# A chain of three transformer blocks on one core: two of the four weight sums of a block product move from VectorE to GpSimd

## The reference

```python
def conv_ffn(h, in_w, conv_w, conv_b, out_w):
    u = causal_dwconv(h @ in_w, conv_w, conv_b)
    g, v = jnp.split(u, 2, axis=-1)
    return (jax.nn.silu(g) * v) @ out_w
```

## Time and profile before

| what | value |
|---|---|
| median of 3 runs | 3161.73 us (3160.71 to 3162.06) |
| the profiled execution | 3163.01 us, its span 3161.2 us, granted TensorE clock 0.996 |
| PE matmuls busy | 3098.6 us, 98% of the span |
| DVE busy | 1332.4 us, 42% |
| ACT busy | 705.6 us, 22% |
| POOL busy | 286.0 us, 9% |
| feed-forward of layer 0, pairs 2 to 21 on PE | 399.73 to 527.41 us |
| feed-forward of layer 1, pairs 2 to 21 on PE | 867.27 to 995.03 us |

### The profile page before, as it was taken

One profiled execution on the slowest core, in us unless ns is written; L12 is line 12 of the kernel. 1 busy time (PEld: TensorE's weight loads), 2 busy tenths in 40 slices (PEclk: granted clock), 3 DMA queues, 4 the chain that ended last, 5 costly groups with the idle time before them and its releaser, 6 DMA issues.

```text
span 3161.2 us, 44989 instructions
## 1 busy us (share of the span) xinstructions
PE 3098.6 (98%) x18322; PEld 2420.7 (77%) x18322; DVE 1332.4 (42%) x2837; ACT 705.6 (22%) x1252; POOL 286.0 (9%) x240
## 2 busy tenths in 40 slices
PE   8999999999999999999999999999999999999998
PEld 7788899888899888998899988888455545544544
DVE  4632289473489455754367544444111111111111
ACT  3621121252221152102220133420111111111111
POOL 0210001070010100001100013200000000000000
PEclk9999999999999999999999999999999999999999
DMA  6543344433244433443254443236899999999996
GB/s 242 160 147 134 120 173 161 160 120 120 87 182 161 157 120 133 169 165 147 94 192 164 155 156 127 83 133 243 349 428 429 428 428 429 428 429 429 428 429 264
DMA packets 72725, 719.43 MB, mean 228 GB/s; under 512 B 8273, under 2 KB 8273, under 8 KB 10753
## 3 DMA queue, kind: packets, MB, share of 16 engines
q1 hardware_dynamic: 70704, 709.93, 56.6%
q0 software_dynamic: 1872, 7.38, 1.0%
HBM read 716.19 MB, written 1.08 MB: 227 GB/s over the span
## 4 chain that ended last, share of the span: by engine, by line
PE 85%; DMA 9%; DVE 4%; ACT 1%; issue 1%; POOL 0%; SPq 0%; DVEq 0%; POOLq 0%; ACTq 0%
PE bank L285 28%; PE bank L2379 11%; PE bank L1399 10%; PE bank L3553 10%; DMA weight_ring<-in_experts 9%; PE bank L304 8%; PE bank L3584 5%; PE bank L3538 3%; PE bank L3530 2%; PE bank L2677 1%; DVE residual L1144 1%; PE bank L487 0%; PE bank L1251 0%; PE bank L1231 0%; PE bank L1698 0%
## 5 line engine op out<-in xcount | busy, mean ns | idle before, releaser
L285 PE MATMUL bank<-normed_residual,weight_ring 128*128 128x256 f32 x2400 | 535.3, 381 | 0.0
L285 PEld LDWEIGHTS bank<-normed_residual,weight_ring 128*128 128x128 f32 x2400 | 452.6, 190 | 66.3 <-issue 7.2
L3637 DVE TENSOR_TENSOR arena<-bank,arena 128x512 f32<-128x512 f32 x32 | 22.1, 691 | 614.3 <-PE bank L3553 614.3
L285 PE MATMUL bank<-arena,weight_ring 128*128 128x256 f32 x1144 | 253.5, 381 | 4.7 <-ACT arena L1758 3.9
L285 PEld LDWEIGHTS bank<-arena,weight_ring 128*128 128x128 f32 x1144 | 217.4, 191 | 34.8 <-issue 4.3
L3553 PE MATMUL bank<-weight_ring,arena 128*64 128x512 f32 x1024 | 227.7, 593 | 3.1 <-DMA weight_ring<-in_experts 3.1
L3553 PE MATMUL bank<-arena 128*64 128x512 f32 x1024 | 225.2, 592 | 2.3 <-DVE arena L3631 2.3
L304 PE MATMUL bank<-gained_residual,weight_ring 128*128 128x256 f32 x896 | 204.2, 388 | 21.5 <-DVE gained_residual L378 12.0
L3584 PE MATMUL bank<-weight_ring,arena 128*64 128x512 f32 x992 | 219.7, 595 | 0.0
L304 PEld LDWEIGHTS bank<-gained_residual,weight_ring 128*128 128x128 f32 x896 | 174.2, 195 | 48.2 <-DVE gained_residual L378 14.0
L3553 PEld LDWEIGHTS bank<-weight_ring,arena 128*64 128x64 f32 x1024 | 72.6, 137 | 152.8 <-issue 138.9
(11 more groups left out here) (460 smaller groups left out, 4397.2 us busy)
## 6 DMA issues: line engine op xcount, KB each, us to landing
weight_ring<-in_stream SPq DMA_DIRECT2D x290, 1024.0 KB, 4.8
weight_ring<-in_experts SPq DMA_DIRECT2D x126, 2048.0 KB, 18.7
arena<-in_experts SPq DMA_DIRECT2D x66, 2048.0 KB, 18.9
arena<-rows POOLq DMA_DIRECT2D x8, 512.0 KB, 6.7
residual<-in_x SPq DMA_DIRECT2D x2, 512.0 KB, 6.3
arena<-in_mem POOLq DMA_DIRECT2D x1, 1024.0 KB, 5.1
out<-gained_residual SPq DMA_DIRECT2D x4, 256.0 KB, 2.3
arena<-in_p POOLq DMA_DIRECT2D x2, 256.0 KB, 2.8
```

What stands on the lines that cost most here:

```text
L285: mm = nc.tensor.matmul(PB[b][:, m * T:m * T + T], l, r, start=(kc == 0), stop=(kc == chunks - 1))
L3637: nc.vector.tensor_tensor(CHID, PB[1][:, :], CSILU, ALU.mult).then_inc(sem["hid_ready"], 1)
```

## The change

All pairs from 3 to 21 go through blocks now (19 of 22; pairs 8, 14 and 20 are new in each layer), so the second linear's units start at n = 19 in place of 16. For the first linear's units POOL makes sums 0 and 2 (ffn_sums_pool) and signals pair_sums; DVE waits for that and makes sums 1 and 3 alone. The second linear's units have all four sums on DVE as before.

```diff
-    return name[:6] == "ffn_in" and p > 2 and p % 6 != 2 or name[:7] == "ffn_out" and p < FFN_OUT_WHOLE
+    return name[:6] == "ffn_in" and p > 2 or name[:7] == "ffn_out" and p < FFN_OUT_WHOLE
...
+        def ffn_sums_pool(pool, l, n):
+
+            u, c = ffn_unit(l, n), FFN_UNITS[n][3]
+            w = W[:, u % SLOTS]
+            pool.wait_ge(arrived[u % SLOTS], 16 * (u // SLOTS + 1))
+            if n >= 2:
+                pool.wait_ge(sem["unit_used"], ffn_unit(l, n - 2) + 1)
+            nc.gpsimd.tensor_tensor(ffn_sums(l, n, 0), w[:, 0:c, hi], w[:, c:2 * c, hi], ALU.add).then_inc(sem["pair_sums"], 1)
+            nc.gpsimd.tensor_tensor(ffn_sums(l, n, 2), w[:, 0:c, lo], w[:, 0:c, hi], ALU.subtract).then_inc(sem["pair_sums"], 1)
+
         def ffn_sums_dve(dve, own, l, n):
...
-            if n >= 2:
+            if n < len(IN_PAIRS):
+                dve.wait_ge(sem["pair_sums"], 2 * len(IN_PAIRS) * l + 2 * n + 2)
+            else:
                 dve.wait_ge(sem["unit_used"], ffn_unit(l, n - 2) + 1)
-            own(nc.vector.tensor_tensor(ffn_sums(l, n, 0), w[:, 0:c, hi], w[:, c:2 * c, hi], ALU.add))
-            nc.vector.tensor_tensor(ffn_sums(l, n, 2), w[:, 0:c, lo], w[:, 0:c, hi], ALU.subtract)
-            own.wait()
+                own(nc.vector.tensor_tensor(ffn_sums(l, n, 0), w[:, 0:c, hi], w[:, c:2 * c, hi], ALU.add))
+                nc.vector.tensor_tensor(ffn_sums(l, n, 2), w[:, 0:c, lo], w[:, 0:c, hi], ALU.subtract)
+                own.wait()
...
             for q in range(11):
+                for p in range(0 if q == 0 else 2 * q + 3, min(2 * q + 5, 22)):
+                    if p in IN_PAIRS:
+                        ffn_sums_pool(pool, l, IN_PAIRS.index(p))
```

More of the change, by code:

```diff
@@ L200 @@
 mem1_ready swept_conv swept_gate conv_mm conv_out
-part_done second_in second_std hn_gate block_ready""".split()
+part_done pair_sums second_in second_std hn_gate block_ready""".split()
 def program(nc, io):
```

## The result

| kernel | median us | lowest to highest | runs |
|---|---|---|---|
| before | 3161.89 | 3160.71 to 3162.49 | 8 |
| changed | 3171.79 | 3170.17 to 3172.87 | 8 |

The ratio is 1.0029, 95% interval 1.0019 to 1.0038: slower by 9.9 us, where the prediction took 0.2% (6.3 us) as the limit of what can be told. No run of one kernel lies in the range of the other. The profiled execution of the changed kernel took 3172.87 us (span 3171.1), 9.86 us more than that of before.

The account below looks back on a forecast made before the run. PE was taken as the limit, with DVE barely keeping up. Terms -3.96 + 2.6 + 1.8 + 4.7 = +5.1 us on the median 3161.73 gave 3166.8 us, bounds 3163 to 3169, range 3161 to 3172.

Parts of the forecast that it names:

- longer POOL sums: Rival: POOL's sums take 1.58 us, not 1.26; starts wait longer, +2.6 us in all, 3169.4 us; chance 0.18.
- Three whole pairs a layer become block pairs: PE in the first linear, both layers: pairs of 6.25 us replace pairs of 6.91, -3.96 us.
- Steady state: Pairs 3 to 19: POOL's sums are ready in time and don't slow DVE; 0 us, cover 2.7 us.
- the waiting copy: Rival: the copy opening DVE's putting together waits for POOL too; 8.4 us in all, 3175 us; chance 0.06.
- Start of a layer: Before pair 2: DVE's sums wait for POOL, delaying the normalised input; PE stands 2.6 us in layer 0, 1.8 in layer 1.
- the slacks of 1.4 and 1.65: Before pair 2, layers 0 and 1: us between the input's first half being ready and PE taking it, in the kernel before.
- over 1.7 us each: Sign expected in the changed profile: how long each of DVE's two sums lasts at a layer's start.
- End of the first linear: Pair 20's added DVE work makes PE wait 2.0 us for "crossed"; +2.4 us a layer, 4.7 in both.
- The second unit's wait: Second linear, second unit: PE waits 0.9 us for DVE's sums, where it was 0.54.
- So PE stands 2.6 us: Layer 0 before pair 2: reciprocal 4.1 us late, less slack 1.4, gives PE 2.6 us of waiting.

Follow-up runs that it names:

- the idle time removed: Changed kernel with DVE's sums of unit 0 moved behind the reciprocal, normalised input and two scalings: 3164.43 us, 1.0008 of before.
- idle time alone: Kernel before plus nine dependent VectorE products on a scratch tile ahead of the reciprocal in each layer: 3171.58 us, 1.0029 of before.
- a shift alone: Kernel before with PE doing the first half of pair 2 twice in both layers, no new idle time: 3169.06 us, 1.0019 of before.

## Why the prediction was right in part

The range, 3161 to 3172, held the time, but at its upper end; the move was forecast as +5.1 us and is +9.9. It lies beyond 0.2%, to which the text gave 0.27, not within, which had 0.70, and beyond the forecast's own bounds, 3163 to 3169, which had 0.61. The range reached so far for longer POOL sums, which didn't come; what came had no term in it, so that the range held is in part luck.

- **Three whole pairs a layer become block pairs, -3.96 us**: right, -1.96 a layer over pairs 3 to 21 without a gap.
- **Steady state, 0 us**: right. POOL's sums take 1.27 us, the copy 0.29 beside them; neither the rival of longer sums nor that of the waiting copy came true, and the run without POOL's sums shows that the help was needed.
- **Start of a layer, 2.6 and 1.8 us of idle time**: right in mechanism. The idle times are 2.61 and 2.40, and the stretch from the statistics +2.78 and +2.43, with 0.36 and 0.32 given back ahead of the statistics. These come sooner because POOL's third addition, without DVE's sums beside it, takes 1.27 us in place of 1.63 and 2.98. The sum used this for POOL, but took the slacks of 1.4 and 1.65 from the trace of before, where PE got its statistics later. In layer 0 this is made up by a reciprocal 0.4 us earlier than forecast, so the hit at 2.6 is in part luck; in layer 1, where PE's statistics come 0.6 us sooner after that addition, it is why 1.8 became 2.40. The sign "over 1.7 us each" for DVE's sums came out as 1.67 and 1.64 in layer 0, and as 2.88 and 0.69 in layer 1, where the first stood through two of POOL's.
- **End of the first linear, 2.4 us a layer**: right in mechanism and place, 1.95 measured; "crossed" ended 535.03 - 522.55 = 12.5 us after pair 20's end (0.2 us before DVE's copy at 522.75), where the sum had 12.75. The second unit's wait, for which the sum had 0.9 in place of 0.54, is 0.56.
- **Left out of the sum: the clock behind the idle time.** The step "So PE stands 2.6 us" took idle time at its length alone. It costs 1.7 us a layer more, 3.4 in both; the runs with the idle time removed, and with it alone, show it. The trace of before had rows that would have warned, two sweeps of the same 40 products:

```profile
608.60 8.90 PE L304 MATMUL bank<-gained_residual,weight_ring 128*128 128x256 f32 x40 [1.00 <-DVE gained_residual L378]
...
850.08 10.59 PE L304 MATMUL bank<-gained_residual,weight_ring 128*128 128x256 f32 x40 [4.46 <-DVE gained_residual L378]
```

Behind 1.00 us of idle time they take 8.90 us; behind 4.46 us, with the clock at 0.50 from 850.1 to 853.5, 10.59: 1.7 us more. Nearer to the forecast's 2.6 and 1.8 us is the conformer part, where 0.50 followed two idle times of 1.82 and 2.00 us. With 1.7 us in both layers the forecast would have been 3170.2 us, though no row of before told that 2.6 or 1.8 us alone suffices.

- **The remaining 1.9 us** come from stages with the same code, with +2.1 in the conformer part alone. There the half-clock stretches are longer, and they begin before PE starts again. Why the clock fell earlier there stays open: neither a shift alone nor earlier falls explain it.

## What to carry to other kernels

An idle time of two to three microseconds on a busy TensorE can have a second price, here 1.7 us in five of six cases: read from the trace what the same group of products takes behind short and long idle times, and put the difference into the forecast with a chance. Work handed to another engine should not stand, with its wait, ahead of what the critical engine needs next: here moving one call behind the norm gave back all that the change lost at the layers' starts. And where a cheaper form of a step moves work to an engine that just keeps up, look at the end of the stage, where the skipped work was the slack.

## What the runs showed of the hardware that was not expected

- Idle times of 2.40 to 2.72 us before pair 2 were followed by a granted clock of 0.50 in each of five cases (changed kernel twice, pair 20 whole once, idle time alone twice), one of 2.25 us was not, and neither was one of 1.66 us before "crossed". The lower clock began 0 to 1.2 us after PE had started again, and pair 2 lost 1.7 us. With all sums on DVE the clock also fell, in both layers, behind two idle times of 1.68 and 1.94 us that came 4 us apart, so no single length decides it here.
- A DVE sum that waits for the port isn't always next: at 867.87 it lasted 2.88 us, through the POOL sums at 867.71 and 868.94, while in layer 0 the two engines took turns. The Trainium skill, page SBUF — State Buffer, section "Who interferes with whom", says that a VectorE instruction with two SBUF inputs contends with a GpSimd instruction that reads SBUF, and calls the shared port pair an exclusive lock. The trace agrees in both layers (1.67 and 2.88 us for a sum that takes 0.69 alone), but who comes next after a wait is not fixed by that.
- With the same code, half-clock stretches behind 2 us and 3.9 us idle times lasted 3.4 us in some profiles and 6.8 in others, which makes 2.1 us between the profiles of before and after. Which of the two it is goes with when the clock fell. Over the ten profiles of this case, at pair 2 and at the idle times of 2, 3.9, 4.5 and 4.5 us (near 706, 723, 850 and 1074 us before), every stretch of 3.4 us began between 0.5 us before and 1.2 us after PE started again, and every one of 6.8 us began 0.6 to 3.0 us before, with PE standing. What sets the moment of the fall is not shown.
